# Down rows requested four turns ahead of their number in a gather stage on one Trainium2 core

## What is computed

```python
def chunk(args):
    xc, ec, gc = args
    u = jnp.take(peer_u, ec, axis=0)
    act = jax.nn.gelu(jnp.einsum('cd,ckd->ck', xc, u))
    vv = jnp.take(peer_v, ec, axis=0)
    return jnp.einsum('ck,ckd->cd', gc.astype(xc.dtype) * act, vv)
```

## Time and profile before

| | us |
|---|---|
| median of three runs | 1525.46 |
| the profiled execution, its own time | 1530.73 |
| its span, first to last instruction | 1528.9 |
| PE (TensorE matmul) busy | 1325.2, 87% |
| VectorE busy | 724.1, 47% |
| POOL (GpSimd) busy | 570.9, 37% |
| ScalarE busy | 304.1, 20% |
| first and last gather request | 289.5 and 1188.8 |

### The profile page before, as it was taken

One profiled execution on the slowest core, in us unless ns is written; L12 is line 12 of the kernel. 1 busy time (PEld: TensorE's weight loads), 2 busy tenths in 40 slices (PEclk: granted clock), 3 DMA queues, 4 the chain that ended last, 5 costly groups with the idle time before them and its releaser, 6 DMA issues.

```text
span 1528.9 us, 13787 instructions
## 1 busy us (share of the span) xinstructions
PE 1325.2 (87%) x4656; PEld 753.3 (49%) x4656; DVE 724.1 (47%) x1642; ACT 304.1 (20%) x735; POOL 570.9 (37%) x531
## 2 busy tenths in 40 slices
PE   6999999567897896895798999899888998999997
PEld 6868689433454563443344455343333344554443
DVE  5125242585764666565765676655535322220001
ACT  1131111331221112221231321111110122411102
POOL 1000000366777667776764556546554100000000
PEclk8899999788998999998899999999999999999999
DMA  9845544589999999999999999999999889688882
GB/s 395 325 172 184 221 164 164 175 302 370 353 354 389 405 408 404 409 398 364 376 410 410 408 409 409 409 409 409 409 410 408 295 306 411 221 253 276 287 301 91
DMA packets 135284, 507.33 MB, mean 332 GB/s; under 512 B 15408, under 2 KB 16304, under 8 KB 133168
## 3 DMA queue, kind: packets, MB, share of 16 engines
q0 software_dynamic: 75456, 293.63, 49.2%
q1 hardware_dynamic: 58320, 208.63, 37.4%
q10 hardware_dynamic: 1440, 4.19, 0.8%
HBM read 505.35 MB, written 1.05 MB: 331 GB/s over the span
## 4 chain that ended last, share of the span: by engine, by line
PE 49%; DMA 21%; another core or an unknown queue 9%; DVE 8%; issue 5%; POOL 4%; ACT 3%; SPq 0%; DVEq 0%; ACTq 0%; POOLq 0%
PE ps_M L843 18%; DMA arena<-in_peer_u,arena 14%; PE ps_M L398 7%; PE ps_T L644 6%; PE ps_T L645 5%; DMA ring<-in_w_second 3%; DMA ring<-in_peer_v,arena 3%; DVE tmp L1877 3%; POOL ring L1111 2%; PE ps_M L408 2%; PE ps_M L590 2%; PE ps_S L419 2%; PE ps_M L619 2%; POOL arena L1098 1%
## 5 line engine op out<-in xcount | busy, mean ns | idle before, releaser
L843 PE MATMUL ps_M<-ring,arena 128*128 128x512 f32 x1088 | 497.5, 600 | 12.5 <-DMA ring<-in_w_second 8.8
L1098 POOL DMA_INDIRECT arena<-in_peer_u,arena x256 | 274.5, 1072 | 252.0 <-DVE tmp L1877 100.0
L1111 POOL DMA_INDIRECT ring<-in_peer_v,arena x256 | 289.3, 1130 | 172.0 <-issue 64.6
L644 PE MATMUL ps_T<-ring,arena 128*128 128x512 f32 x436 | 240.5, 635 | 106.0 <-ACT arena L1249 54.7
L843 PEld LDWEIGHTS ps_M<-ring,arena 128*128 128x128 f32 x1088 | 203.2, 192 | 251.3 <-issue 241.4
L645 PE MATMUL ps_T<-ring,arena 128*128 128x512 f32 x436 | 233.4, 618 | 0.0
L1877 DVE SCALAR_TENSOR_TENSOR tmp<-arena,merged 128x1024 f32<-128x1024 f32 x128 | 156.8, 1225 | 143.2 <-DMA arena<-in_peer_u,arena 127.1
L1877 DVE SCALAR_TENSOR_TENSOR tmp<-arena 128x1024 f32<-128x1024 f32 x128 | 156.3, 1221 | 66.9 <-DMA arena<-in_peer_u,arena 51.2
L644 PEld LDWEIGHTS ps_T<-ring,arena 128*128 128x128 f32 x436 | 77.5, 199 | 201.3 <-issue 140.3
L645 PEld LDWEIGHTS ps_T<-ring,arena 128*128 128x128 f32 x436 | 86.9, 199 | 111.9 <-issue 111.9
L398 PE MATMUL ps_M<-hT,ring 128*128 128x256 f32 x576 | 129.9, 385 | 1.3 <-ACT hT L1262 1.3
(11 more groups left out here) (257 smaller groups left out, 1092.7 us busy)
## 6 DMA issues: line engine op xcount, KB each, us to landing
ring<-in_w_second SPq DMA_DIRECT2D x276, 512.0 KB, 4.6
arena<-in_w_ada POOLq DMA_DIRECT2D x12, 2048.0 KB, 10.8
ring<-in_w_in SPq DMA_DIRECT2D x46, 512.0 KB, 8.3
ring<-in_w_pq SPq DMA_DIRECT2D x32, 512.0 KB
ring<-in_w_out SPq DMA_DIRECT2D x16, 512.0 KB, 4.0
ring<-in_w_br SPq DMA_DIRECT2D x16, 384.0 KB, 3.1
arena<-in_peer_u,arena POOLq DMA_INDIRECT x256
ring<-in_peer_v,arena POOLq DMA_INDIRECT x256
```

The lines of the kernel that those rows point to most:

```text
L644: low = mm(twin[:, 0:512], dg[:, i % 8, :], v_ring[n % VR][:, 0:512], start=first, stop=last)
L843: m = mm(bank, left[c], w[:, c, :], start=first and c == 0, stop=last and c == 1)
L1098: pool.indirect_dma_start(u_ring[:, n % UR, :], None, A["peer_u"][0], bass.IndirectOffsetOnAxis(ap=expert[:, u % 3, k:k + 1], axis=0))\
L1111: pool.indirect_dma_start(v_ring[n % VR], None, A["peer_v"][0], bass.IndirectOffsetOnAxis(ap=expert[:, u % 3, k:k + 1], axis=0))\
```

## The change

The POOL loop issues down row n + 4 where it issued down row n, and so also the first four down rows of each phase in the last four turns of the phase ahead. The wait for the index table moves from the head of the phase to just before its first up row, behind one down row. The up rows keep their places, both rings their sizes, and the consumers their order.

```diff
 RING = 12
 UR, VR = 6, 8
+AHEAD = 4
 ARENA = 28964
...
             for phase in range(-1, NU):
-                if phase + 1 < NU:
-                    pool.wait_ge(idx_ready, phase + 2)
                 for k in range(TOPK):
-                    if phase >= 0:
-                        gather_v(phase, k)
+                    if k < TOPK - AHEAD and phase >= 0:
+                        gather_v(phase, k + AHEAD)
+                    elif k >= TOPK - AHEAD and phase + 1 < NU:
+                        gather_v(phase + 1, k + AHEAD - TOPK)
                     if phase + 1 < NU:
+                        if k == 0:
+                            pool.wait_ge(idx_ready, phase + 2)
                         gather_u(phase + 1, k)
```

## The result

The changed kernel took 1554.4 us, median of four runs (1546.3 to 1557.2), against 1526.9 us for four runs of the kernel before: a ratio of 1.015, 95% interval 1.011 to 1.019. Beside the last experiments it was timed again on one chip, with the same ratio, 1.015 (1.013 to 1.017). It is slower by 23 to 27 us. The forecast was 1543.5, 18 us slower, in a range from 1517 to 1572. Ratios are formed from undisturbed executions alone and not from the medians, so the two differ by up to 0.3%; one of ten executions of the first experiment took 6440 us and is left out of its ratio. The profiled execution took 1557.2 us, its span 1555.4.

The account below looks back on a forecast made before the run. It took late up rows to bound the gather stage, with DMA full from 780 us. Terms 0 - 2 + 20 + 0 + 0 = +18 us on the median of 1525.5 gave 1543.5 us, range 1517 to 1572.

Parts of the forecast that it names:

- the count of requests: POOL's queue: count and bytes of requests stay the same, 256 up and 256 down; cost 0.
- the index waits: POOL's index-table waits (51.8 us in 9) mostly vanish but become waits for PE's takes; 0.
- item 2: Start of the gather: the first up row of the next set loses one request ahead of it; -2 us.
- the prediction's own last sentence: Sign of being wrong: the first stretches keep their GB/s, or the full stretch shows holes.
- Item 3, phases 0 to 2: Up requests held to four turns beyond PE's take delay each phase's last dot; 5.1, 1.2 and 3.7 us.
- Item 3, phases 4 to 7: Same late last dots, less cover from a shorter queue; 1, 1.6, 4 and 5.8 us.
- Item 4, the full stretch: From 780 to 1204 us some 12 tiles, 15 us, stay in hand, so DMA stays full; cost 0.
- Rival B: Much slower: 5.1 us holes in each of phases 9 to 15, 36 us on top of 18, 1579 us; chance 0.14.
- Rival A: Faster: earlier down requests fill DMA holes worth 10.1 us, up rows no later in effect, 1513.5 us; chance 0.16.
- Rival C: No change: DMA-bound from 480 us, late requests repaid by unused engines and a shorter queue, 1525.5 us; chance 0.16.

Follow-up runs that it names:

- the last experiments: Beside the kernel before (1529.2 us): changed kernel again 1.015; up requests waiting for row n-4, old order 1.003, down rows two turns early 1.004; the last experiment 1.007.
- the first experiment: Kernel before plus one wait: the up row's request also waits until row n-4 is taken; 1537.3 us against 1530.4, ratio 1.002.
- e7: Changed loop with a lead of three turns in place of four, up rows tied to row n-5; 1515.6 us against 1511.5, ratio 1.004.
- e5: Changed loop with a lead of three turns, up row's request also waiting until row n-4 is taken; 1525.3 us against 1511.5, ratio 1.010.
- the set with the tie to row n-4: Kernels whose up requests wait until row n-4 is taken, against the kernel before: down rows no turns early 1.003, two 1.004, three 1.010, four (changed) 1.015.
- The tie alone: Kernel before, no down row early, up request also waiting until row n-4 is taken; ratio 1.002, on another occasion 1534.5 us against 1529.2, ratio 1.003.
- the last experiment: Kernel before with only the first four down rows early, then down row n-2 in the place of turn n; 1541.1 us against 1529.2, ratio 1.007.
- e8: Kernel before with down rows later, row n-2 in the place of turn n; 1509.1 us against 1511.5, ratio 0.998.

## Why the prediction was right, and where it was not

**The direction and the size of the whole.** The price of +18 us stands beside 23 to 27 measured, and the first links of its mechanism are in the rows: POOL waits for takes where it waited for dots, VectorE waits for up rows, DMA has gaps, the stage's end moves and the rest follows at its old length. The items on the count of requests and on the index waits held; of the 2 us of item 2, 0.9 came (PE's first take at 330.9 before, 330.0 after).

That the sum came so near is luck. Up to phase 8 the items stand at 22.4 - 2 = 20.4 us (taken as 18), and 6.8 were measured; after it at 0, and 19.9 were measured. By the prediction's own last sentence it was wrong twice: the first stretch kept its 346 GB/s, and the full stretch shows holes (394 GB/s, not 408). Its wait for takes also stands at the down line and not at the up line, and the last request goes out 28 us later (1217.0 us, 1188.8 before), not 18.

**Item 3, phases 0 to 2.** Charged with 5.1 + 1.2 + 3.7 us and the start with -2; measured -1.5 at the beginning of phase 4. The step that failed is that PE's takes were held at their old times. They moved: in the kernel before, ScalarE had waited 123.1 us in 12 times for PE products by an unknown releaser, twice about 10 us within phase 0; in the profile after it was 38.0 us in 5. Two copies of PE's query products in phase 0 began 7.3 and 5.6 us after the product's last matmul had ended, and within 0.2 us of it in the profile after; PE's next rows began right after these copies (354.7 and 367.0 us), as ScalarE makes their diagonals behind them. Row 11 came 11.8 us earlier and the later request with it. The experiment with the lead in these phases alone confirms the cost of nothing, not the reason; whether the change or the chance of one profile took these delays away was not separated.

**Item 3, phases 4 to 7.** Charged with 12.4 us, measured 8.3 (9.7 with the second profile of the changed kernel). Two thirds of the charge, and not a clean measure: the profile before has late copies of 13.0 and 16.2 us in these phases.

**Item 4, the full stretch: cost 0.** This is the term that was mis-sized: 19.9 us from the start of phase 8, where item 3 stops. Phase 8 itself, which before ran from 739 to 790 us, was priced by no item ahead of 780 us and cost 10.8 us; it begins right behind PE's longest wait for a diagonal, 19.7 us, and DMA went at 351 GB/s in it, not full. From phase 9 on it is 9.1 us. The argument counted tiles in hand in a steady run, 12 x 1.28 = 15 us against four turns of 3.84 us, and left out what happens once in each phase. The last up row may only be asked for when row 11 is taken; it lands behind the queue; then come dot, weights and diagonals. If PE has taken its remaining rows by then, it takes nothing, and POOL, which now asks for nothing without a take, goes quiet too. The measured means fit this account: 8.6 us from take to last dot before, 14 after, with four turns of 3.84 us for PE's remaining rows, and PE's wait for diagonals twice as long. They do not prove it: 12.7 us went with 0.4%, 13.8 in e7 with 0.4%, 14.0 in e5 with 1.0%, and the kernels outside the set with the tie to row n-4 do not follow it. I also read "taken by PE (or VectorE)" and then priced PE alone: 49.3 us of POOL's waits, 12 times, are for rows that VectorE adds, 1.0 us before.

**Rival B** had nearly the right place and a wrong price: holes in the full stretch, 16.7 us in all and not 36, with the largest single loss in phase 8, ahead of its phases 9 to 15. **Rival A's** gain did not come as a faster kernel: the bandwidth from 290 to 480 us is 346 GB/s in both. **Rival C** did not come: the time is clear of no change. Its premise was a quick landing. The Trainium skill's page "DMA: Bandwidth & Descriptors" (section "Anatomy of one DMA — SWDGE (gpsimd) path") gives a fit by which such a tile takes about 3.2 us, an estimate from the page's figures. No row agrees: from request to dot it is 5.3 us in phase 0 above, 4.5 in the earlier trace rows, and 13.9 in the earlier trace rows, with some ten tiles queued. The measurement decides; so a lead in turns has to be held against the time from request to dot under load.

**What stays open.** That early down rows make the same tie dearer is shown by the kernels at the tie to row n-4; whether they do so by POOL's time (1.24 us a request) or by their place in the DMA queues was not separated. No kernel took the 10.8 us of phase 8 apart. The tie alone never came alone: its wait held down rows back too. And the last experiment shows that part of what these profiles hold is not explained by the order of requests.

## What to carry to other kernels

One in-order queue that issues two streams ties each stream to the other's slowest buffer: moving one stream ahead by k of its N slots lets the other go at most N - k turns ahead of the consumer's last take, whatever its own ring allows (here 8 - 4 = 4). Look which stream is waited for before giving the other a head start, and count the room not in steady state alone but also at the point where the loop closes on itself, here the last row of a phase, whose dot the next phase's weights need, and where one kind of phase gives way to another, here phase 8. The cost of lost lead sets in: here two turns were free, the third cost 4 to 6 us, the fourth some 20 more. And check a forecast by its parts: this one came near in sum with both halves wrong.

## What was not expected of the hardware

ScalarE's waits with an unknown releaser. At 709.94 us of the kernel before ScalarE copies a query product of PE's after 27.11 us of idling, whose last matmul the trace shows ending before 694; SyncE's load behind the same product goes in the same moment. They sum to 123.1 us (12 times) before, 38.0 (5) after, 128.5 (9) in the last experiment. The share of an unknown queue in the chain that ended last is 9% before and 1% after.

They go with the chip, as far as the record tells (it names none for the profiles before and after). Read as the time from the end of a query product's last matmul (or of ScalarE's last work, where that is later) to the start of its copy, over the 32 products and where it is over 1 us, the delay sums to 60.0 us in the kernel before, 14.5 and 26.8 in the two profiles of the changed kernel, 66.8 in the last experiment, and 19 to 50 in the six other profiles of that experiment's chip. In all four profiles of the other chip (e5 to e8) it is zero, whatever the order of the requests, and there the kernel before takes 1511.5 us in place of 1529.2 to 1530.4. That the delays are what this difference of 18 to 19 us consists of is not shown. No experiment here was made on them. They are of the size of what was sought, so a kernel of this kind is judged by timed runs on one chip and not by one profile.

The granted clock. In the full stretch its mean was 0.98 before and 0.93 after, with PE busy for 376 of 424 us and 390 of 454; the page's sum of PE's busy time is 1330.0 us instead of 1325.2, for as many matmuls. So by this sum a lower clock explains at most 4.8 us of the 26.5 by which the span grew; how much of that was hidden in waits was not separated.
